# Two transformer blocks on one core: a low part and a memory key in another order, square roots and a Silu ahead of an eviction, last transposes half a product earlier

## Reference

```python
def first_block(x, ...):
    for l in range(2):
        mix = hybrid_mixer(x, ...)          # delta rule 384 | convolution 256 | attention 384 columns
        x = layer_norm(ALPHA * x + mix, ...)
        ff = swiglu(x, ...) if l == 0 else moe_swiglu(x, ...)   # 2816 wide; 8 experts, top 2, 3584 wide
        x = layer_norm(ALPHA * x + ff, ...)
    return x

def second_block(x, mem, ...):
    x = x + 0.5 * swiglu_ffn(rms_norm(x, ffn1_norm), ...)
    h = rms_norm(x, mix_norm)
    q_a, k_a, v_a, q_i, k_i, w_i, u_s, q_m, gates = split(h @ w_in)
    o_a = indexed_sparse_attention(rms_norm(q_a), rms_norm(k_a), v_a, q_i, k_i, w_i, rel_bias) @ w_o_a
    y_s = gelu(s5_layer(u_s, ...))          # complex diagonal scan over 256 steps
    glu_a, glu_b = split(y_s @ w_glu)
    o_b = glu_a * sigmoid(glu_b)
    o_m = memory_attention(rms_norm(q_m), rms_norm(m_k), m_v) @ w_o_m   # m_k, m_v from mem
    g = sigmoid(gates)                      # 3 x 1024 columns
    x = x + (g[0] * o_a + g[1] * o_b + g[2] * o_m) @ w_out
    x = x + 0.5 * swiglu_ffn(rms_norm(x, ffn2_norm), ...)
    return rms_norm(x, final_norm)
```

## Time and profile before

| | us |
|---|---|
| three runs | 2251.81, 2253.58, 2254.72 |
| median | 2253.58 |
| the profiled execution, its own time | 2255.03 |
| its span in the profile | 2253.0 |
| PE busy | 2161.3 |
| DVE busy | 1568.7 |
| ACT busy | 1204.1 |
| mean granted clock of PE, share of full | 0.984 |

### The profile page before, as it was taken

One profiled execution on the slowest core, in us unless ns is written; L12 is line 12 of the kernel. 1 busy time (PEld: TensorE's weight loads), 2 busy tenths in 40 slices (PEclk: granted clock), 3 DMA queues, 4 the chain that ended last, 5 costly groups with the idle time before them and its releaser, 6 DMA issues.

```text
span 2253.0 us, 31915 instructions
## 1 busy us (share of the span) xinstructions
PE 2161.3 (96%) x12155; PEld 1818.1 (81%) x12155; DVE 1568.7 (70%) x1619; ACT 1204.1 (53%) x1198; POOL 161.3 (7%) x234
## 2 busy tenths in 40 slices
PE   8989999998899999999999999999899997999997
PEld 7978888897778888888888888888688876877886
DVE  3655453465488898989898988988765439767453
ACT  4133443313267777777777777677564323655442
POOL 1200000320300000000000000000075010000000
PEclk9999999999899999999999999999999998999999
DMA  9123555422379999999999999999756553525552
GB/s 346 61 94 122 187 187 186 140 69 94 106 279 371 353 362 349 359 349 360 349 363 346 362 371 349 366 350 354 271 163 191 192 136 112 187 81 172 186 186 75
DMA packets 244882, 537.24 MB, mean 238 GB/s; under 512 B 18006, under 2 KB 128640, under 8 KB 244416
## 3 DMA queue, kind: packets, MB, share of 16 engines
q1 hardware_dynamic: 240656, 521.11, 65.0%
q0 software_dynamic: 3168, 9.07, 1.6%
q10 hardware_dynamic: 976, 5.91, 0.6%
HBM read 534.71 MB, written 1.31 MB: 238 GB/s over the span
## 4 chain that ended last, share of the span: by engine, by line
PE 83%; DVE 10%; issue 3%; ACT 3%; DMA 1%; DVEq 0%; SPq 0%; ACTq 0%
PE bank L1262 9%; PE bank L1264 9%; PE bank L1263 9%; PE bank L1389 7%; PE bank L1390 7%; PE bank L1393 7%; PE bank L1014 6%; PE bank L1404 4%; PE bank L1409 4%; PE bank L1405 4%; PE bank L1205 3%; PE bank L1531 2%; DVE weights_lo L2309 2%; PE bank L1364 1%; DVE arena L2512 1%
## 5 line engine op out<-in xcount | busy, mean ns | idle before, releaser
L2309 DVE TENSOR_TENSOR weights_lo<-ring_data,weights_hi 128x2048 fp32r<-128x2048 f32 x336 | 759.4, 2289 | 89.7 <-ACT weights_hi L1995 88.2
L1995 ACT ACTIVATE weights_hi<-ring_data 128x2048 fp32r<-128x2048 f32 x336 | 637.2, 1919 | 163.2 <-DMA ring_data<-in_moe_w 162.5
L1389 PE MATMUL bank<-weights_hi,xg_hi 128*128 128x512 f32 x896 | 352.1, 393 | 4.0 <-DVE arena L2719 2.6
L1390 PE MATMUL bank<-weights_hi,xg_lo 128*128 128x512 f32 x896 | 349.3, 390 | 0.0
L2304 DVE TENSOR_TENSOR weights_lo<-ring_data,weights_hi 128x2048 fp32r<-128x2048 f32 x98 | 226.3, 2340 | 51.9 <-ACT weights_hi L1782 51.9
L1393 PE MATMUL bank<-weights_lo,xg_hi 128*128 128x512 f32 x896 | 239.7, 390 | 0.0
L1263 PE MATMUL bank<-weights_lo,xT_hi 128*128 128x512 f32 x584 | 228.8, 392 | 0.0
L1262 PE MATMUL bank<-weights_hi,xT_hi 128*128 128x512 f32 x520 | 206.5, 397 | 1.3 <-DVE xT_lo L2297 0.6
L1264 PE MATMUL bank<-weights_hi,xT_lo 128*128 128x512 f32 x520 | 203.5, 391 | 0.0
L1389 PEld LDWEIGHTS bank<-weights_hi,xg_hi 128*128 128x128 f32 x896 | 168.4, 188 | 38.4 <-issue 3.0
L1393 PEld LDWEIGHTS bank<-weights_lo,xg_hi 128*128 128x128 f32 x896 | 168.3, 188 | 35.1
(11 more groups left out here) (485 smaller groups left out, 3200.7 us busy)
## 6 DMA issues: line engine op xcount, KB each, us to landing
ring_data<-in_moe_w SPq DMA_DIRECT2D x672, 512.0 KB, 4.3
ring_data<-in_ffn_w_in SPq DMA_DIRECT2D x88, 512.0 KB, 4.5
ring_data<-in_w_in SPq DMA_DIRECT2D x70, 512.0 KB, 4.5
ring_data<-in_ffn_w SPq DMA_DIRECT2D x66, 512.0 KB, 4.0
ring_data<-in_ffn_w_out SPq DMA_DIRECT2D x44, 512.0 KB, 3.8
ring_data<-in_w_out SPq DMA_DIRECT2D x24, 512.0 KB, 4.4
ring_data<-in_w_in SPq DMA_DIRECT2D x8, 396.0 KB, 4.0
ring_data<-in_w_in SPq DMA_DIRECT2D x8, 390.0 KB, 5.6
```

The costliest lines, as they stand in the source:

```text
L1389: mm(o, xg_hi[:, k, :], e_hi(at)[:, r], start=k == 0, stop=False)
L1390: mm(o, xg_lo[:, k, :], e_hi(at)[:, r], start=False, stop=False)
L1995: nc.scalar.activation(e_hi(at), ring_data[:, e_slot(at), :], ACT.Copy).then_inc(ring.hi_done, 1)
L2309: v.tensor_tensor(e_lo(at), ring_data[:, e_slot(at), :], e_hi(at), ALU.subtract).then_inc(ring.lo_done, 1)
```

## The change

Five reorderings; no arithmetic is added or removed.

1. Dense stages: the last `step` is written out. `down` of chunk 9 is cut into its two halves of 12 matmuls, and `turn` of chunk 10 goes between them.
2. Experts: in the last pass `turn_h(3)` goes from ahead of down slot (3,0) to ahead of (2,3).
3. Mixers, ACT: the two square roots and the convolution's Silu go ahead of the eviction of the last projection.
4. Branches, PE and ACT: projection 4 goes ahead of the memory key's transposes; on ACT `gate_high(0)` and the eviction of projection 4 go ahead of the key's eviction.
5. Branches, DVE: `gx_lo`, with its waits for `gx_hi` and for the use of the last projection's slot, goes from behind the whole turn into the turn by +1 of group 0, behind its four multiplications.

```diff
--- before.py
+++ after.py
@@ -1283,19 +1283,21 @@
                         i = nc.tensor.transpose(bank[f.up_banks[c % 2][j]][:, P * q:P * q + P], f.h[:, c % 2, j, P * q:P * q + P], ident)
                 i.then_inc(f.hT_psum, 1)
 
-            def down(f, c, r=0):
+            def down(f, c, r=0, parts=(0, 1)):
                 at = f.down_at(c)
-                pe.wait_ge(f.ring.lo_done, f.m0 + at + 1 + r * 6)
-                pe.wait_ge(f.hT_done, f.c0 + c + 1 + r * 2)
+                if 0 in parts:
+                    pe.wait_ge(f.ring.lo_done, f.m0 + at + 1 + r * 6)
+                    pe.wait_ge(f.hT_done, f.c0 + c + 1 + r * 2)
                 w_hi, w_lo = (w.rearrange("p (f d) -> p f d", f=2) for w in (f.hi_slot(f.n0 + at), f.lo_slot(f.n0 + at)))
-                for q in range(2):
+                for q in parts:
                     for j in range(f.tiles):
                         t = slice(P * j, P * j + P)
                         for d in range(2):
                             cd = slice(512 * d, 512 * d + 512)
                             i = three(bank[f.y_banks[j][d]][:, :], f.hT_hi[:, c % 2, q, t], f.hT_lo[:, c % 2, q, t],
                                       w_hi[:, q, cd], w_lo[:, q, cd], False, False, skip_group_check=True)
-                i.then_inc(f.ring.used, 1)
+                if 1 in parts:
+                    i.then_inc(f.ring.used, 1)
 
             def down_by_bank(f):
 
@@ -1324,8 +1326,15 @@
                 with pe.Fori(0, f.bodies) as i:
                     step(f, 1, r + i)
                     step(f, 2, r + i)
-                for c in range(2 * f.bodies + 1, f.chunks):
+                for c in range(2 * f.bodies + 1, f.chunks - 1):
                     step(f, c, r)
+                last = f.chunks - 1
+                up(f, last, 0, r)
+                turn(f, last - 1, r)
+                up(f, last, 1, r)
+                down(f, last - 1, r, (0,))
+                turn(f, last, r)
+                down(f, last - 1, r, (1,))
 
             def dense(f, u):
 
@@ -1337,7 +1346,6 @@
                 up(f, 0, 1)
                 pe.wait_ge(sem("y_zeroed"), u + 1)
                 steps(f)
-                turn(f, f.chunks - 1)
                 down_by_bank(f)
 
             def moe():
@@ -1446,7 +1454,7 @@
                             pe.wait_ge(sem("moe_hT"), it * 4 + 3)
                             if not is_last:
                                 gather(it + 1)
-                        if part == ("next", 0, 1) or (is_last and part == ("down", 3, 0)):
+                        if part == ("next", 0, 1) or (is_last and part == ("down", 2, 3)):
                             if is_last:
                                 pe.wait_ge(sem("moe_h"), it * 4 + 4)
                             turn_h(3)
@@ -1565,14 +1573,13 @@
                 block_inputs(range(4))
                 project(3)
                 block_inputs(range(4, NS))
-
+                project(4)
                 pe.wait_ge(sem("bu_act"), NS)
                 for t in range(2):
                     for j in range(TT):
                         i = nc.tensor.transpose(bk(4, 2, T)[:, t, P * j:P * j + P], mkv[:, j, P * t:P * t + P], ident)
                 i.then_inc(sem("pe_stage"), 1)
-                for m in range(4, 6):
-                    project(m)
+                project(5)
                 pe.wait_ge(sem("act_stage"), stage("mkT_act"))
                 proj2_out(pe, 2)
                 for h in range(IH):
@@ -1935,6 +1942,12 @@
                 act.wait_ge(sem("gdn_psum"), 7 * l + 7)
                 act.wait_ge(sem("decay_causal"), 5 * l + 3)
                 a_(forget[0:H, :], bk(7, T)[0:H], ACT.Copy, "gdn_act")
+                act.wait_ge(sem("mix_var"), 2 * l + 1)
+                a_(std[:, 0:TT], mv[:, :, 1], ACT.Sqrt, "mix_std", bias=LN_EPS)
+                act.wait_ge(sem("mix_var"), 2 * l + 2)
+                a_(rr12[:, :], ss12[:, :], ACT.Sqrt, "mix_std", scale=1.0 / HD, bias=NORM_EPS)
+                act.wait_ge(sem("conv_normed"), l + 1)
+                a_(mixed[:, :, GW:GW + CW], mixed[:, :, GW:GW + CW], ACT.Silu, "conv_out")
                 project(len(PROJ) - 1)
 
                 def weights(h):
@@ -1953,12 +1966,6 @@
                 def mixed_out(t, b, d, inc):
                     a_(actT[:, t, :], bk(b, 2, T)[:, d], ACT.Copy, inc, scale=pcol[:, l, R_MIX + t:R_MIX + t + 1])
 
-                act.wait_ge(sem("mix_var"), 2 * l + 1)
-                a_(std[:, 0:TT], mv[:, :, 1], ACT.Sqrt, "mix_std", bias=LN_EPS)
-                act.wait_ge(sem("mix_var"), 2 * l + 2)
-                a_(rr12[:, :], ss12[:, :], ACT.Sqrt, "mix_std", scale=1.0 / HD, bias=NORM_EPS)
-                act.wait_ge(sem("conv_normed"), l + 1)
-                a_(mixed[:, :, GW:GW + CW], mixed[:, :, GW:GW + CW], ACT.Silu, "conv_out")
                 weights(0)
                 act.wait_ge(sem("mixed_turned"), 5 * l + 1)
                 mixed_out(3, 0, 0, "act_steps")
@@ -2143,10 +2150,10 @@
                     a_(bu[:, j], bk(4 + j % 4, 2, T), ACT.Copy, "bu_act")
                     if j == 3:
                         project(3)
+                gate_high(0)
+                project(4)
                 act.wait_ge(sem("pe_stage"), stage("mkT_psum"))
                 a_(mkT[:, :, :], bk(4, 2, T), ACT.Copy, "act_stage")
-                gate_high(0)
-                project(4)
                 gate_high(1)
                 project(5)
                 for h in range(IH):
@@ -2884,6 +2891,10 @@
                         st.do(tt(t1, bi, s, ALU.mult))
                         st.do(tt(t2, bi, c, ALU.mult))
                         st.do(tt(br, br, c, ALU.mult))
+                        if (sign, g) == (1, 0):
+                            dve.wait_ge(sem("gx_hi"), 1)
+                            dve.wait_ge(ring2.used, N_GATE)
+                            v.tensor_tensor(gx_lo[:, :, :], actT[:, :, :], gx_hi[:, :, :], ALU.subtract).then_inc(sem("gx_lo"), 1)
                         st.settle()
                         st.do(tt(br, br, t1, ALU.add if sign < 0 else ALU.subtract))
                         i = tt(bi, t2, t0, ALU.subtract if sign < 0 else ALU.add)
@@ -2900,10 +2911,6 @@
                                 for q in range(2):
                                     st.do(v.tensor_tensor_scan(bu[:, j, q, :], m, bu[:, j, q, :], 0.0, ALU.mult, ALU.add))
                             st.settle()
-
-                dve.wait_ge(sem("gx_hi"), 1)
-                dve.wait_ge(ring2.used, N_GATE)
-                v.tensor_tensor(gx_lo[:, :, :], actT[:, :, :], gx_hi[:, :, :], ALU.subtract).then_inc(sem("gx_lo"), 1)
 
                 dve.wait_ge(sem("idx_rel"), IH)
                 proj2_out(dve, 2)
```

## The result

| | before | after |
|---|---|---|
| median of four runs each, same chip, us | 2254.15 | 2232.86 (2228.76 to 2235.70) |
| ratio after/before, 95% interval | | 0.9904 (0.9892 to 0.9916) |
| profiled execution, own time / span | 2255.03 / 2253.0 | 2235.65 / 2233.6 |

A forecast was written before the change was run, and what follows sets the result against it. PE, busy for 96% of the span, bounds the kernel; time is won only where it stands still or runs at half clock. 5.4 + 1.7 + 10.1 + 5.6 = 22.8 us, giving a median of 2230.8, range 2228.6 to 2239.5.

The forecast's parts named there:

- head start: Mixers: with roots and Silu ahead of the last eviction, DVE starts `head(0)` 3.3 us sooner in each; bounds 2.5 and 3.4.
- clock: Mixers, behind the scores: PE idles less, so the granted clock stays up, worth 2.4 and 1.1 us; rival that it falls, 0.17.
- PE itself is late next: Mixers: once the Silu's wait is gone, PE's own scores set the pace, letting DVE start `head(0)` 3.3 us sooner.
- the slack: Mixers: the Silu ends at 148.6, leaving 1.1 us to the last projection's eviction at 149.78.
- The rule on table loads: Mixers, ACT: about 1.38 us of drain behind each load, 2.66 in all, would leave 0.3 us instead of 1.1.
- Dense stages: Three dense stages: 12 matmuls (2.8 us) cover the 1.63 us wait for the last low part; 1.8 us each, 5.4 together.
- The neighbour rule: See who comes next once a wait is gone; third dense stage: `turn` finds its `h_done` with 0.7 us to spare.
- Experts: Last pass of the experts: 12 matmuls (2.8 us) cover the 1.5 us wait at L1404; 1.7 us, bounds 1.0 and 1.9.
- is still under the cover: Experts: one low part of a weight (2.29 us) ahead of the tile's in DVE's queue still fits behind 2.8 us of matmuls.
- Branches: Branches, to the end of the gates: moved key and `gx_lo` bring that end 5.6 us sooner; bounds 3.5 and 6.2.
- The start of the gates: Branches: PE's gates start 3.8 us sooner, since the 2.1 at L1572 and a half clock behind it go.
- the term of 1.7 for the half clock behind L1572: Branches, ahead of the gates: the half clock (0.51) behind the 2.1 us wait at L1572 goes with it, worth 1.7 us.

The follow-up runs named there:

- parts 1 and 2: Kernel before plus only the earlier last transposes of the three dense stages and of the experts; 0.9958 (0.9941 to 0.9975) of the kernel before.
- parts 4 and 5: Kernel before plus only the memory key behind projection 4 and `gx_lo` inside the turn of group 0; 0.9977 (0.9963 to 0.9991).
- part 5: Kernel before plus only `gx_lo` inside the turn of group 0, memory key in its old place; 0.9964 (0.9949 to 0.9979).
- part 4: Kernel before plus only the memory key behind projection 4, `gx_lo` still behind the whole turn; 0.9996 (0.9986 to 1.0006).
- part 3 alone: Kernel before plus only the two square roots and the Silu ahead of the last projection's eviction in both mixers; 0.9958 (0.9941 to 0.9974).
- second profile of the changed kernel: The changed kernel measured once more, with nothing altered; 2234.64 us, 0.9896 (0.9877 to 0.9916) of the kernel before.
- the late variances: Changed kernel with the delta-rule output's squares computed five times instead of once on DVE, ahead of the variances, in both mixers; 0.9928 (0.9912 to 0.9945).
- the Silu behind: Changed kernel with the Silu alone put back behind the last projection's eviction in both mixers, roots still ahead; 0.9899 (0.9883 to 0.9916).
- the early low parts: Changed kernel with low parts of the gate weights earlier in DVE's order and high parts 8 and 9 ahead of the heads' root on ACT; 2226.69 us, 0.9874.
- the kernel with filler matmuls: Kernel before plus two unused matmuls on PE ahead of each of the two waits between `scores(1)` and `turn_p(0)`, both mixers; 0.9987 (0.9977 to 0.9996).

## Why the prediction was right, and where it was not

**What bounds the kernel, and the mixers.** Against the profile before, right to 0.1 us in every term: head start 3.3 each, clock 2.4 and 1.1. The head start repeats: `turn_p(0)` comes 3.86 to 3.87 us behind `scores(0)` in both mixers of all four profiles that have part 3 as it is. The 2.4 is in part the luck of one profile, from which forecast and measurement both start. Four other kernels leave the mixers as they were (parts 1 and 2, parts 4 and 5, part 5, part 4), and there mixer 0 takes 14.16 to 14.40 us from `scores(0)` to the first `out`, and mixer 1 14.20 to 14.40, at a mean clock of 0.88; only in the profile before is it 15.37 at 0.78. Windows, mixer 0, the kernel before, then parts 4 and 5:

```profile
150.52:165.89 15.37, 11.70 (x64) 10.28 (x64) 10.37 (x25) 9.70 (x24) 0.00 (x0) 0.78 0.22 69
```

```profile
149.81:163.97 14.16, 10.49 (x64) 9.17 (x64) 10.36 (x25) 9.70 (x24) 0.00 (x0) 0.88 0.25 75
```

Against these four the clock is worth 1.2 to 1.4 us in each mixer, and the mixers give 9.1 to 9.5 in all instead of 10.2; the times of part 3 alone, 9.5, can't tell the two apart. "PE itself is late next" held as well: the slack was 1.3 to 1.4, not 1.1. The rule on table loads that spoke against this edit (the Trainium skill, ScalarE: Activation LUTs, What ACT_TABLE_LOAD costs) is contradicted by all twelve profiles: no 1.38 us of drain on either side of a load, but 0.01 to 0.02 us between it and its neighbours wherever they wait for nothing else. Had the drain been there, the slack would have been as thin as that page makes it.

**Dense stages.** Forecast 1.8 each, measured 1.8, 1.98 and 1.85. The neighbour rule was right too: in `ffn2` DVE's product is ready at 2213.51 + 0.88 = 2214.4 and the transposes start at 2215.16, 0.8 of slack (forecast 0.7).

```profile
2215.16 0.60 PE L1283 MATMUL bank<-consts_sb,arena 128*128 128x128 f32 x4
```

```profile
2213.51 0.88 DVE L2325 SCALAR_TENSOR_TENSOR arena<-bank,small,params 128x256 f32<-128x256 f32 x2 [1.58 <-ACT params L1794]
```

**Experts: a step that held only with an early DMA.** 1.7 was forecast; in the profile of the changed kernel the place itself gave 1.0, the lower bound, and the stretch as a whole 0.68. The sentence was that a low part of a weight in DVE's queue "is still under the cover". ACT, DVE and PE, after:

```profile
1592.36 1.92 ACT L2002 ACTIVATE weights_hi<-ring_data 128x2048 fp32r<-128x2048 f32 x1 [1.96 <-DMA ring_data<-in_moe_w]
```

```profile
1594.30 2.29 DVE L2316 TENSOR_TENSOR weights_lo<-ring_data,weights_hi 128x2048 fp32r<-128x2048 f32 x1 [1.58 <-ACT weights_hi L2002]
1596.51 0.68 DVE L2732 TENSOR_TENSOR hT_lo<-bank,hT_hi 128x512 fp32r<-128x512 f32 x1
```

```profile
1593.49 0.60 PE L1385 MATMUL bank<-consts_sb,arena 128*128 128x128 f32 x4
...
1597.33 0.49 PE L1412 MATMUL bank<-weights_hi,hT_hi 128*128 128x512 f32 x1 [0.49 <-DVE hT_lo L2732]
```

The cover runs to 1596.84. DVE's low part begins 0.8 behind the start of the transposes, because ACT's high part waited 1.96 for the DMA of that weight, and the tile's own 0.68 comes on top of its 2.29. In the second profile of the changed kernel the same low part begins ahead of the transposes (1593.06), and no wait is left:

```profile
1592.67 2.29 DVE L2316 TENSOR_TENSOR weights_lo<-ring_data,weights_hi 128x2048 fp32r<-128x2048 f32 x1 [0.65 <-ACT weights_hi L2002]
```

From the transposes to the first `Y_hi` product it takes 11.77 us in the first profile, 11.03 in the second and in those of the late variances and of the Silu behind, 11.37 in that of the early low parts, against 12.76 before: 1.0, 1.4 or 1.7. So the forecast's 1.7 is what the move gives when the weight comes early; the sum had no term for when the operation ahead in the queue can begin. Putting `hT_lo` ahead of that low part would take the DMA out of it; it was not tried.

**Branches.** The size at the end was right by DVE's clock: 5.51 from the turn (forecast 5.6), with a stand of 4.54 at slot 2 (forecast 5) and one of 2.63 for `gx_lo` (2 to 4). The start of the gates was wrong: 3.8 us sooner was forecast, 2.24 came, because the term of 1.7 for the half clock behind L1572 was not tied to that stand. Behind the turn it is 3.18 sooner; the rest, 0.94, is that the turn itself began later. I had read the half clock ahead of the gates as a consequence of the stand at L1572 alone. The stand is gone, and a half clock is there all the same, a little earlier in the stage and with PE never idle. And in the profile of parts 1 and 2 alone, where the stand of 2.12 us at this place is kept, the clock behind it is 1.00 (1859 to 1864) and the half clock falls ahead of it (0.76 from 1848 to 1855). The start cost nothing of the forecast, as part 4 alone shows, but the late turn cost 0.94 of the 5.5.

**The sum.** 22.8 forecast, 19.4 in the profiled execution. Of the 3.4 missing, 1.0 is in the experts, 0.7 of it by the late DMA; 0.94 and 1.31 are the half clock ahead of DVE's turn and behind the gates, and 0.76 is in stretches ahead of the mixers' scores that the change does not touch; the dense stages gave 0.6 more than forecast. The 1.31 is absent in the second profile; 1.2 to 1.4 us at this place stand in five of the twelve profiles and nothing in the others, whatever the edit. I take such stretches to fall by chance; it is argued from twelve profiles, and their trigger was not isolated. The 19.4 are those of one execution of 2235.65 us, 2.8 above the median of its kernel; by the medians 21.3 of the 22.8 came.

## To carry to other kernels

Before an edit that starts the bound engine sooner, ask which engine's fixed order sets the end of that stage, and measure from that engine's first instruction: part 4 began the gates 2.7 us sooner for nothing, part 5 gave 5.1 without it. Behind a gap, add the lower clock to the price of the gap; dummy matmuls in the gap measure that term by itself. When a result must come out from under a cover, sum the queue ahead of it, its own duration, and the earliest moment at which the queue can move.

## What the runs showed of the hardware

The half clock can fall with PE busy throughout, by the profile's modelled ends of matmuls. Part 3 alone leaves the branches as they were, and still:

```profile
1838.54:1843.54 5.00, 5.00 (x29) 3.79 (x29) 1.54 (x2) 2.48 (x6) 0.00 (x0) 0.66 0.66 210
```

against the same 5 us of the kernel before:

```profile
1850.72:1855.72 5.00, 5.00 (x36) 4.24 (x36) 1.88 (x3) 2.48 (x6) 0.00 (x0) 1.00 0.63 209
```

PE runs the same order of instructions without a stand in both; ahead of the stretch stand 32 matmuls of four columns each. In the kernel with part 5 alone, where nothing differs up to that point either, it is 0.50 over such a window; in the kernel with filler matmuls it is 1.00. The turn of DVE, which waits for what PE makes here, then begins 28.5 us into the stage where the clock holds, and up to 30.7 where it falls; in two profiles where it falls over 26 us into the stage, behind parts 1 and 2 alone and with the Silu behind, the turn still begins at 28.5. This makes a stretch of the same code 2 us longer or shorter from one kernel to the next, as much as most of the edits in this case are worth.
